# Attention by query tiles of 16 rows and 8 columns over stripes of keys, in a diffusion step kernel

## The chip, the core and the metric

The kernel runs on one NeuronCore of a Trainium2 chip. A core has five engines with instruction queues of their own: TensorE (PE in the profile, its weight loads PEld), VectorE (DVE), ScalarE (ACT), GpSimd (POOL) and SyncE (SP, which here issues every DMA). Each works through its queue in order and waits for the others by semaphores. The metric is the time of one execution on the device in microseconds (us).

## The reference

One layer of a hybrid network, run on 256 context tokens and 1024 latent tokens (a grid of 16 rows of 64), all in float32. Only the attention is touched by the change:

```python
def _neighbourhood_attention(q, k, v, k_ctx, v_ctx, rpb):   # latent queries
    row_start = jnp.clip(r - kh // 2, 0, rows - kh)          # kh = 8 of 16 rows
    row_idx = row_start[:, None] + jnp.arange(kh)[None, :]
    col_start = jnp.clip(c - NA_KW // 2, 0, GRID_W - NA_KW)  # 16 of 64 columns
    col_in = (c[None, :] >= col_start[:, None]) & (c[None, :] < col_start[:, None] + NA_KW)
    s_loc = jnp.einsum('brqhd,brjkhd->bhrqjk', qg, kg).astype(jnp.float32) * scale
    s_loc = jnp.where(col_in[None, None, None, :, None, :],
                      s_loc + bias[None].astype(jnp.float32), NEG_INF)
    s_ctx = jnp.einsum('brqhd,bchd->bhrqc', qg, k_ctx).astype(jnp.float32) * scale
    p = jax.nn.softmax(jnp.concatenate([s_loc.reshape(B, H, rows, GRID_W, n_loc), s_ctx], axis=-1), axis=-1)
    ...
```

There are 8 heads of 64. The latent queries see a window of 8 rows and 16 columns of latent keys and, in the same softmax, 256 cached keys. The context queries see the 256 context keys alone. Around the attention stand one input projection (with the gates of three branches), a pooling and a convolution branch, an output projection and a gated feed-forward part.

## The kernel before

The program has three parts: a front (modulation, norm, the first 18 column units of the input projection and the two small mixers), the attention beside which the remaining 21 units of gate columns are projected, and a rear (output projections and feed-forward).

Float32 products are made of split operands: a high part (`hi`, rounded to the fp32r format) and the rest (`lo`). `products` (L149) issues three matmuls for each piece. A unit of the input projection has 24 pieces: three chunks (512, 512 and 256 tokens) of 8.

In the front, ACT's `evacuate` (L625) copies V (units 6 to 9), K (10 to 13) and Q (14 to 17) out of PSUM into `evac`. V is transposed to token order and stored by `store_tokens` (L316), the latent part once for each of 4 column windows and 2 parities into `v_windows`; K and Q are stored to `kT` and `qT`.

The attention (`attention_engines`, L1104) goes through 80 steps, `s = 10 h + n`: for each head `h` eight latent query tiles (`n` = 0 to 7) of 8 rows and 16 columns, and two tiles of context queries (`n` = 8, 9). Each latent tile sees 12 rows and 32 columns of keys (`LOCAL` = 384) and the 256 cached keys. A step's work is spread over several later steps:

- PE, in step s: `scores(s)` (two local matmuls, L1287, and two for the cached keys, L1292), then half of the gate pieces of this step, `turn(s - 2)` (transposes of the probabilities, L1301), the other gate pieces, `value(s - 3)` (L1315). A step has 5 or 6 gate pieces.
- DVE, in step s: `maximum(s)` (L1448 to L1452), `total(s - 1)` (L1460, L1462), `gather(s - 4)` (L1484), `lower(s - 2)` (L1469), and what is named below.
- ACT, in step s: `gate_out` of a gate chunk that has ended, `exponential(s)` (the cached part, L1367, then the local, L1369), `upper(s - 2)` (L1378), the split of a new weight unit (`split`, L1338).
- POOL, in step s: `normalise(s - 1)` (L1538), the low part of a new weight unit (`lower`, L1514).

`scores(s)` has to wait until DVE has read the local scores of the tile before (`max_step`), and for the cached part until ACT has made its exponentials (`past_ready`): there is one buffer of each.

Between these stand the operations of which each head needs one set. For the next head: KA on ACT (L1344, high part of the keys) and then KB on POOL (L1520, low part) at n = 2 (3 in the first head); QS on ACT (five copies, L1348) and DVE (five, L1432) at n = 5; VV at n = 8; the bias tables on POOL (`tables`, L1531, three additions at n = 4 and three at n = 1). For the output of a head: V stands in the stationary operand with its two parts, so that the output rows come in two halves of the partitions. `lower_rows` (ACT, L1385) copies the second half down to OLO, `add_rows` (DVE, L1490) adds it to OT, and SP stores the sum. This is done at n = 9 for the first 512 tokens, and at n = 4 of the next head for the other 768.

The lines in the loops of ACT and DVE that set this place are the same:

```python
                if n == 9 and h < HEADS:
                    lower_rows(h, 0)
                if n == TIMES + 1 and h > 0:     # TIMES = 3
                    lower_rows(h - 1, 1)
```

## Time and profile before

| | |
|---|---|
| median of 3 runs | 1873.34 us (1871.3 to 1873.45) |
| profiled execution | 1871.09 us, its span 1869.3 us |
| front, to about 330 us | PE busy 320.6 of 330 us |
| attention, 360 to 750 us | PE busy 388.1 of 390 us, DVE 234.8, ACT 222.6, POOL 198.5 |
| rear, 750 to 1869 us | PE busy 1109.7 of 1119 us |
| granted TensorE clock | 1.00 in the attention, 0.998 over the span (2.4 GHz is 1) |

The span runs from the first to the last instruction of the profiled execution. A busy time of PE counts each matmul to its modelled end; since matmuls overlap, the start of one to the start of the next says more than a duration.

### The profile page before, as it was taken

The page shows a single profiled execution, that of the slowest core. Times are in us where ns is not written, and L with a number is a line of the kernel's source. Part 1 is how long each engine was busy: PE and PEld are TensorE (multiplying, and loading weights), DVE is VectorE, ACT ScalarE, POOL GpSimd, SP SyncE. Part 2 cuts the span into 40 slices and gives each one's busy share as a digit, 9 for nine tenths or more (in the row PEclk, how much of TensorE's full clock was granted, in tenths as well). Part 3 has the DMA queues.
Part 4 walks back from the last instruction along what each step waited for, and adds up shares of the span by engine and source line. Part 5 has one row for each costly group of instructions (what it writes and reads, how often), then busy time and mean ns, then how long its engine had stood idle before and what let it go on. Part 6 is the DMA issues. An engine that isn't in the chain of part 4 may idle for free.

```text
span 1869.3 us, 27109 instructions
## 1 busy us (share of the span) xinstructions
PE 1847.3 (99%) x10106; PEld 1587.0 (85%) x10106; DVE 1145.8 (61%) x2142; ACT 758.2 (41%) x1444; POOL 543.7 (29%) x407
## 2 busy tenths in 40 slices
PE   8999999999999999999999999999999999999998
PEld 3788888888888888888888888888888888888898
DVE  4799996156566655366317855554434434789984
ACT  5612232355555564454313522222222222545464
POOL 0000000455555552144532144444344441000000
PEclk9999999999999999999999999999999999999999
DMA  8472545464444532756532222221222224866665
GB/s 325 161 221 62 148 128 192 120 151 115 112 119 112 126 95 75 239 169 185 180 116 68 82 77 96 96 84 58 74 74 74 74 74 150 283 209 224 210 212 204
DMA packets 243466, 260.52 MB, mean 139 GB/s; under 512 B 50696, under 2 KB 182280, under 8 KB 242312
## 3 DMA queue, kind: packets, MB, share of 16 engines
q1 hardware_dynamic: 243336, 258.80, 44.8%
q8 instruction: 81, 1.33, 0.3%
q14 instruction: 49, 0.40, 0.1%
HBM read 196.09 MB, written 62.65 MB: 138 GB/s over the span
## 4 chain that ended last, share of the span: by engine, by line
PE 90%; DVE 4%; DMA 2%; ACT 2%; issue 1%; POOL 0%; SPq 0%; ACTq 0%; DVEq 0%; POOLq 0%
PE ps_all L152 68%; PE ps_all L2452 5%; PE ps_all L2454 4%; PE ps_all L2453 4%; PE ps_all L1315 2%; PE ps_all L1301 2%; DVE mod_acc L825 1%; PE ps_all L1287 1%; DMA wmod_then_mixers<-w_mod_dram 1%; PE ps_all L1292 1%; PE ps_all L537 1%; DMA wmod_block<-w_mod_dram 1%; DVE Y L3114 0%; POOL KB L1520 0%; PE ps_all L2486 0%
## 5 line engine op out<-in xcount | busy, mean ns | idle before, releaser
L152 PE MATMUL ps_all<-AH,w_hi 128*128 128x512 f32 (+1 forms) x1376 | 493.7, 359 | 2.4 <-ACT gate_rows L1360 1.3
L152 PE MATMUL ps_all<-AH,w_lo 128*128 128x512 f32 (+1 forms) x1376 | 483.1, 351 | 0.0
L152 PE MATMUL ps_all<-AL,w_hi 128*128 128x512 f32 (+1 forms) x1376 | 483.0, 351 | 0.0
L152 PEld LDWEIGHTS ps_all<-AH,w_lo 128*128 128x128 f32 x1376 | 259.9, 189 | 36.0
L152 PEld LDWEIGHTS ps_all<-AH,w_hi 128*128 128x128 f32 x1376 | 260.2, 189 | 34.3 <-DVE AL L909 2.0
L152 PEld LDWEIGHTS ps_all<-AL,w_hi 128*128 128x128 f32 x1376 | 260.5, 189 | 30.1
L3033 DVE TENSOR_TENSOR quarter<-ps_all,quarter 128x512 f32<-128x512 f32 x140 | 96.6, 690 | 176.6 <-PE ps_all L152 174.6
L2881 POOL TENSOR_TENSOR slot_lo<-w_pair,slot_hi 128x512 fp32r<-128x512 f32 x96 | 129.9, 1378 | 174.0 <-ACT slot_hi L2654 174.0
L152 PE MATMUL ps_all<-AH,slot_hi 128*128 128x256 f32 (+1 forms) x384 | 129.5, 337 | 0.0
L152 PE MATMUL ps_all<-AL,slot_hi 128*128 128x256 f32 (+1 forms) x384 | 129.2, 336 | 0.0
L152 PE MATMUL ps_all<-AH,slot_lo 128*128 128x256 f32 (+1 forms) x384 | 129.1, 336 | 0.0
L2881 POOL TENSOR_TENSOR w_lo<-w_pair,w_hi 128x512 fp32r<-128x512 f32 x64 | 85.4, 1356 | 114.4 <-ACT w_hi L2654 114.4
L1469 DVE TENSOR_TENSOR PT<-ps_all,PT 128x384 fp32r<-128x384 f32 (+1 forms) x144 | 63.7, 479 | 79.7 <-ACT PT L1378 79.6
L1538 POOL TENSOR_SCALAR prob<-prob,softmax_cols 128x640 f32<-128x640 f32 (+1 forms) x80 | 60.5, 756 | 130.5 <-DVE softmax_cols L1462 125.4
L1367 ACT ACTIVATE prob<-ps_all,softmax_cols 128x256 f32<-128x256 f32 x80 | 38.0, 474 | 137.4 <-DVE softmax_cols L1452 123.9
L845 DVE SCALAR_TENSOR_TENSOR xT_then_mixers<-wmod_then_mixers,cols,xT_then_mixers 128x1295 f32<-128x1295 f32 x60 | 89.4, 1573 | 0.0
L2452 PE MATMUL ps_all<-AH 128*128 128x512 f32 (+1 forms) x248 | 86.9, 350 | 1.1 <-DVE AL L3069 1.1
L1514 POOL TENSOR_TENSOR w_lo<-w_raw,w_hi 128x1024 fp32r<-128x1024 f32 x21 | 50.5, 2404 | 124.6 <-ACT w_hi L1338 124.6
L2454 PE MATMUL ps_all<-AH,AL 128*128 128x512 f32 (+1 forms) x248 | 86.3, 348 | 0.0
L2453 PE MATMUL ps_all<-AL,AH 128*128 128x512 f32 (+1 forms) x248 | 86.3, 348 | 0.0
L2452 PE MATMUL ps_all<-AH,w_hi 128*128 128x512 f32 (+1 forms) x236 | 83.9, 355 | 0.0
L2454 PE MATMUL ps_all<-AH,w_lo 128*128 128x512 f32 (+1 forms) x236 | 83.3, 353 | 0.0
(309 smaller groups left out, 4084.6 us busy)
## 6 DMA issues: line engine op xcount, KB each, us to landing
w_raw<-w_in_dram SPq DMA_DIRECT2D x42, 512.0 KB
w_pair<-w_gu_dram SPq DMA_DIRECT2D x20, 1024.0 KB, 5.3
hidden_in<-hidden SPq DMA_DIRECT2D x77, 256.0 KB, 3.5
wmod_then_mixers<-w_mod_dram SPq DMA_DIRECT2D x19, 1024.0 KB, 8.0
hidden<-quarter SPq DMA_DIRECT2D x50, 256.0 KB, 2.1
branch_and_gates<-gates SPq DMA_DIRECT2D x16, 768.0 KB, 4.4
w_down_rows<-w_down_dram SPq DMA_DIRECT2D x44, 256.0 KB, 3.7
gates<-gate_rows SPq DMA_DIRECT2D x42, 256.0 KB, 2.5
```

Source lines behind the costliest of these rows:

```text
L152: mm = nc.tensor.matmul(out, w, a[:, k, cols[0]:cols[1]], start=(first and part == 0), stop=(last and part == 2))
L845: nc.vector.scalar_tensor_tensor(conv[:, t, :], glu[:, t, k:k + CV], w, conv[:, t, :], ALU.mult, ALU.add).then_inc(conv_step, 1)
L1301: mm = nc.tensor.transpose(psT[:, turned_at(j):turned_at(j) + P], prob[:, s % 3, j * P:(j + 1) * P], g.ident[:, :])
L1367: nc.scalar.activation(pr[:, LOCAL:PCOLS], psS_past, ACT.Exp, bias=c[:, 2:3], accum_out=c[:, 4:5]).then_inc(past_ready, 1)
L1469: nc.vector.tensor_tensor(PT[:, s % 2, j0:j1, P:2 * P], psT[:, turned_at(j0):turned_at(j0) + (j1 - j0) * P].rearrange("p (j n) -> p j n", ...
L1514: nc.gpsimd.tensor_tensor(W.lo[:, u % 2, :], W.raw[:, :], W.hi[:, u % 2, :].bitcast(F32), ALU.subtract).then_inc(W.lo_ready, 1)
L1538: nc.gpsimd.tensor_scalar(pr[:, a:PCOLS], pr[:, a:PCOLS], c[:, 5:6], 1.0, ALU.mult, ALU.mult).then_inc(normal, 1)
L2452: nc.tensor.matmul(out, wh, th, start=first, stop=False)
L2453: nc.tensor.matmul(out, wh, tl, start=False, stop=False)
L2454: return nc.tensor.matmul(out, wl, th, start=False, stop=last)
L2881: nc.gpsimd.tensor_tensor(tiles4(lo), in_pair(p, idx), tiles4(hi.bitcast(F32)), ALU.subtract).then_inc(s_lo, 1)
L3033: nc.vector.tensor_tensor(temp[TEMP[out][side]][:, :], g.ps_all[:, product_bank(p, source), :], temp[TEMP[first][side]][:, :], ALU.add).th ...
```

## The change

Keys, values and queries of the latent tokens are kept in stripe order: stripe w holds the 16 rows of columns 8w to 8w + 7, which are 128 tokens. The front's copy out of PSUM writes this order, so that transposes and stores follow it, and `v_windows` with its eight stores for each V unit is gone. A query tile is one stripe. It sees its own stripe and the neighbours: three blocks of 128 keys, and two for the tiles at the grid's sides (`n` = 0 and 7). The blocks are contiguous in K and V, so QS is made by one copy on ACT and one operation on DVE. There are two bias tables a head instead of six, double buffered, made at n = 6 of the head before; their 16 loads are issued at n = 1 and 2. V holds 12 blocks instead of 20. Since a tile now covers all rows, no half of a head's output is complete before its eighth tile: OT is double buffered, and `lower_rows`, `add_rows` and the store are done in three parts (512, 512 and 256 tokens) at n = 2, 3 and 4 of the next head (the store a step later).

The diff, cut to its core:

```diff
-TROWS, TCOLS = 8, 16
-WROWS, WCOLS = 12, 32
-COL0 = (0, 8, 24, 32)
-KIND = (0, 1, 1, 2)
-KINDS = 3
-SPAN = WCOLS + TCOLS
-WINDOWS = len(COL0) * ROWS * WCOLS // P
-V_CTX, V_PAST = WINDOWS, WINDOWS + CTX // P
+TCOLS = 8
+STRIPES = GW // TCOLS
+REACH = 3 * TCOLS
+V_CTX, V_PAST = STRIPES, STRIPES + CTX // P
 V_BLOCKS = V_PAST + PAST // P
...
-                for n, kc in enumerate(COL0):
-                    for parity in range(2):
-                        sp.dma_start(v_windows[n, parity, :, :, col:col + P], vt[parity * GW + kc:parity * GW + kc + WCOLS, 0:LAT // P, :]).then_inc(tok_stored, 16)
-                sp.dma_start(g.d["v"][LAT:T, col:col + P].rearrange("(t p) n -> p t n", p=P), vt[:, 8:10, :]).then_inc(tok_stored, 16)
+                sp.dma_start(g.d["v"][:, col:col + P].rearrange("(t p) n -> p t n", p=P), vt[:, :, :]).then_inc(tok_stored, 16)
...
-                    nc.scalar.activation(evac[:, u % 2, a:b], ps[:, 0:b - a], ACT.Copy).then_inc(a_free, 1)
+                    if c < 2:
+                        out = evac[:, u % 2, 0:LAT].rearrange("p (s r c) -> p s r c", s=STRIPES, c=TCOLS)[:, :, a // GW:b // GW, :]
+                        nc.scalar.activation(out, ps.rearrange("p (r s c) -> p s r c", s=STRIPES, c=TCOLS), ACT.Copy).then_inc(a_free, 1)
+                    else:
+                        nc.scalar.activation(evac[:, u % 2, a:b], ps[:, 0:b - a], ACT.Copy).then_inc(a_free, 1)
...
-LOCAL = WROWS * WCOLS
+LOCAL = ROWS * REACH
 PCOLS = LOCAL + PAST
-HALVES = ((0, LAT // 2), (LAT // 2, T))
-HALF_TILES = (4, QT)
+PARTS = ((0, LAT // 2), (LAT // 2, LAT), (LAT, T))
+PART_TILES = (STRIPES, STRIPES, QT)
 
 
 def tile_plan(n):
 
-    return divmod(n, len(COL0)) if n < LAT // P else None
+    return [s for s in (n - 1, n, n + 1) if 0 <= s < STRIPES] if n < STRIPES else None
+
+
+def local_at(n):
+
+    return LOCAL - P * len(tile_plan(n))
 
...
-    half, group = plan
-    return [(j, len(COL0) * group + half + j) for j in range(3)], [(3, V_PAST), (4, V_PAST + 1)]
+    return [(3 - len(plan) + j, s) for j, s in enumerate(plan)], [(3, V_PAST), (4, V_PAST + 1)]
...
             def load_b(h, half):
-                if h:
-                    sp.wait_ge(*tables_ready(h - 1, half))
-                else:
-                    sp.wait_ge(b_cleared, half + 1)
-                for r in range(TROWS):
-                    row = TROWS * half + r
+                if half == 0:
+                    if h:
+                        sp.wait_ge(*tables_ready(h - 1))
+                    else:
+                        sp.wait_ge(b_cleared, 1)
+                for row in range(half * ROWS // 2, (half + 1) * ROWS // 2):
                     first = window_start(row)
-                    at = first - half * KH // 2
-                    sp.dma_start(bias_src[r * TCOLS:(r + 1) * TCOLS, half, at:at + KH, :], rpb_rows(g, h, first - row + KH - 1)).then_inc(b_in[half], 16)
...
-                for at, src in ((0, g.v_windows), (V_CTX, g.d["v"][LAT:T, :]), (V_PAST, g.d["cache_v"])):
+                for at, src in ((0, g.d["v"]), (V_PAST, g.d["cache_v"])):
...
-            def store_out(h, half):
-                sp.wait_ge(out_ready, 2 * h + half + 1)
-                a, b = HALVES[half]
-                sp.dma_start(out_rows[h * 64:h * 64 + 64, a:b], OT[0:64, a:b]).then_inc(out_stored, 16)
+            def store_out(h, part):
+                sp.wait_ge(out_ready, 3 * h + part + 1)
+                a, b = PARTS[part]
+                sp.dma_start(out_rows[h * 64:h * 64 + 64, a:b], OT[0:64, h % 2, a:b]).then_inc(out_stored, 16)
...
-                    if n in (1, 4):
-                        load_b(h + 1, n // 4)
+                    if n in (1, 2):
+                        load_b(h + 1, n - 1)
...
-                if n == 9 and h < HEADS:
-                    store_out(h, 0)
-                if n == TIMES + 1 and h > 0:
-                    store_out(h - 1, 1)
+                if h > 0 and n in (3, 4, 5):
+                    store_out(h - 1, n - 3)
...
-                at = 2 * plan[1] + plan[0] if plan else n
-                q = QS[:, b, at * P:(at + 1) * P]
+                q = QS[:, b, n * P:(n + 1) * P]
                 if plan:
-                    r0, c0 = plan[0] * KH // 2, COL0[plan[1]]
                     if s:
                         pe.wait_ge(max_step, 2 * b0(s))
                     for m, K in enumerate((KA, KB)):
-                        keys = K[:, b, 0:LAT].rearrange("p (r c) -> p r c", c=GW)[:, r0:r0 + WROWS, c0:c0 + WCOLS]
-                        nc.tensor.matmul(psS_local.rearrange("p (i j) -> p i j", j=WCOLS), q, keys, start=(m == 0), stop=(m == 1))
+                        nc.tensor.matmul(psS_local[:, local_at(n):LOCAL], q, K[:, b, plan[0] * P:(plan[-1] + 1) * P], start=(m == 0), stop=(m == 1))
                 k0 = T if plan else LAT
...
-                    for out, src in by_tiles(QS[:, b, :], kq_src):
-                        nc.scalar.activation(out, src, ACT.Copy, scale=DH ** -0.5).then_inc(q_hi, 1)
+                    nc.scalar.activation(QS[:, b, :], kq_src[:, 0:T], ACT.Copy, scale=DH ** -0.5).then_inc(q_hi, 1)
...
-            def lower_rows(h, half):
-                act.wait_ge(summed_v, h * QT + HALF_TILES[half])
-                if 2 * h + half:
-                    act.wait_ge(out_ready, 2 * h + half)
-                a, b = HALVES[half]
-                nc.scalar.activation(OLO[:, 0:b - a], OT[64:P, a:b], ACT.Copy).then_inc(olo_ready, 1)
+            def lower_rows(h, part):
+                act.wait_ge(summed_v, h * QT + PART_TILES[part])
+                if 3 * h + part:
+                    act.wait_ge(out_ready, 3 * h + part)
+                a, b = PARTS[part]
+                nc.scalar.activation(OLO[:, 0:b - a], OT[64:P, h % 2, a:b], ACT.Copy).then_inc(olo_ready, 1)
...
-                if n == 9 and h < HEADS:
-                    lower_rows(h, 0)
-                if n == TIMES + 1 and h > 0:
-                    lower_rows(h - 1, 1)
-            lower_rows(HEADS - 1, 1)
+                if h > 0 and n in (2, 3, 4):
+                    lower_rows(h - 1, n - 2)
+            lower_rows(HEADS - 1, 2)
 
...
-                half, group = plan
-                if group == 0:
-                    dve.wait_ge(*tables_ready(s // QT, half))
+                h, a = s // QT, local_at(n)
+                if n == 0:
+                    dve.wait_ge(*tables_ready(h))
+                seen = bias[:, b, 1, P:LOCAL] if n == 0 else bias[:, b, 1, 0:2 * P] if n == STRIPES - 1 else bias[:, b, 0, :]
                 nc.vector.tensor_reduce(c[:, 1:2], psS_past, AX, ALU.max).then_inc(max_step, 1)
-                nc.vector.tensor_tensor_reduce(prob[:, s % 3, 0:LOCAL], psS_local, bias[:, half, KIND[group], :],
+                nc.vector.tensor_tensor_reduce(prob[:, s % 3, a:LOCAL], psS_local[:, a:LOCAL], seen,
...
-            def add_rows(h, half):
-                a, b = HALVES[half]
-                rows = OT[0:64, a:b]
-                dve.wait_ge(olo_ready, 2 * h + half + 1)
+            def add_rows(h, part):
+                a, b = PARTS[part]
+                rows = OT[0:64, h % 2, a:b]
+                dve.wait_ge(olo_ready, 3 * h + part + 1)
...
-                if n == 9 and h < HEADS:
-                    add_rows(h, 0)
-                if n == TIMES + 1 and h > 0:
-                    add_rows(h - 1, 1)
-            add_rows(HEADS - 1, 1)
+                if h > 0 and n in (2, 3, 4):
+                    add_rows(h - 1, n - 2)
+            add_rows(HEADS - 1, 2)
 
...
-            def tables(h, half):
-                pool.wait_ge(b_in[half], 16 * TROWS * (h + 1))
-                if h:
-                    pool.wait_ge(max_step, 2 * (b0((h - 1) * QT + 4 * half + 3) + 1))
-                for kind in range(KINDS):
-                    seen = bias_src[:, half, :, TCOLS // 2 * kind:TCOLS // 2 * kind + WCOLS]
-                    nc.gpsimd.tensor_tensor(bias[:, half, kind, :].rearrange("p (i j) -> p i j", j=WCOLS), seen[:, :, ::-1],
-                                            col_mask[:, kind, :].rearrange("p (a j) -> p a j", a=1).broadcast_to([P, WROWS, WCOLS]), ALU.add).then_inc(table_ready, 1)
+            def tables(h):
+                b = h % 2
+                pool.wait_ge(b_in, 16 * ROWS * (h + 1))
+                if h >= 2:
+                    pool.wait_ge(max_step, 2 * (h - 1) * NL)
+                seen = bias_src[:, :, ::-1].rearrange("p r (s c) -> p s r c", c=TCOLS)
+                for kind in range(2):
+                    mask = col_mask[:, kind, :].rearrange("p (s a c) -> p s a c", a=1, c=TCOLS).broadcast_to([P, 3, ROWS, TCOLS])
+                    nc.gpsimd.tensor_tensor(bias[:, b, kind, :].rearrange("p (s r c) -> p s r c", r=ROWS, c=TCOLS), seen, mask, ALU.add).then_inc(table_ready, 1)
 
...
-                if n == 1 and 0 < h < HEADS:
-                    tables(h, 1)
                 if h + 1 < HEADS:
                     if n == (2 if h else 3):
                         prepare("k", h + 1)
-                    elif n == 4:
-                        tables(h + 1, 0)
+                    elif n == 6:
+                        tables(h + 1)
                     elif n == 8:
                         prepare("v", h + 1)
```

On ACT, these rows are from the place in the second head (h = 1, counted from 0) where KA is made: before, from the exponentials of n = 2 to those of n = 4.

```order
L1367 ACTIVATE prob,softmax_cols<-ps_all,softmax_cols 128x256
L1369 ACTIVATE prob,softmax_cols<-prob,softmax_cols 128x384
L1378 ACTIVATE PT<-ps_all 128x3x128
L1378 ACTIVATE PT<-ps_all 128x2x128
L1344 ACTIVATE KA<-kq_src 128x1536
L1367 ACTIVATE prob,softmax_cols<-ps_all,softmax_cols 128x256
L1369 ACTIVATE prob,softmax_cols<-prob,softmax_cols 128x384
L1378 ACTIVATE PT<-ps_all 128x3x128
L1378 ACTIVATE PT<-ps_all 128x2x128
L1360 ACTIVATE gate_rows<-ps_all,cols 128x256
L1367 ACTIVATE prob,softmax_cols<-ps_all,softmax_cols 128x256
```

And in the changed kernel at the same place:

```order
L1353 ACTIVATE prob,softmax_cols<-ps_all,softmax_cols 128x256
L1356 ACTIVATE prob,softmax_cols<-prob,softmax_cols 128x384
L1365 ACTIVATE PT<-ps_all 128x2x128 x2
L1331 ACTIVATE KA<-kq_src 128x1536
L1372 ACTIVATE OLO<-OT 64x512
L1353 ACTIVATE prob,softmax_cols<-ps_all,softmax_cols 128x256
L1356 ACTIVATE prob,softmax_cols<-prob,softmax_cols 128x384
L1365 ACTIVATE PT<-ps_all 128x3x128
L1365 ACTIVATE PT<-ps_all 128x2x128
L1372 ACTIVATE OLO<-OT 64x512
L1346 ACTIVATE gate_rows<-ps_all,cols 128x256
L1353 ACTIVATE prob,softmax_cols<-ps_all,softmax_cols 128x256
```

A copy to OLO stands right behind KA, another behind `upper` of the next step, and the third behind the split of a weight unit (where one falls there).

On DVE, before, the same head from the maximum of n = 3 to that of n = 4:

```order
L1469 TENSOR_TENSOR PT<-ps_all,PT 128x3x128
L1469 TENSOR_TENSOR PT<-ps_all,PT 128x2x128
L1448 TENSOR_REDUCE softmax_cols<-ps_all 128x1
L1449 ISA prob,softmax_cols<-ps_all,bias 128x384
L1449 ISA softmax_cols 128x1
L1452 TENSOR_SCALAR softmax_cols<-softmax_cols 128x1
L1460 TENSOR_TENSOR softmax_cols<-softmax_cols 128x1
L1462 RECIPROCAL softmax_cols<-softmax_cols 128x1
L1484 TENSOR_REDUCE OT<-ps_all 128x128
L1469 TENSOR_TENSOR PT<-ps_all,PT 128x3x128
L1469 TENSOR_TENSOR PT<-ps_all,PT 128x2x128
L1448 TENSOR_REDUCE softmax_cols<-ps_all 128x1
```

And in the changed kernel from the addition at the end of n = 2 to the maximum of n = 4:

```order
L1472 TENSOR_TENSOR OT<-OT,OLO 64x512
L1432 TENSOR_REDUCE softmax_cols<-ps_all 128x1
L1433 ISA prob,softmax_cols<-ps_all,bias 128x384
L1433 ISA softmax_cols 128x1
L1436 TENSOR_SCALAR softmax_cols<-softmax_cols 128x1
L1444 TENSOR_TENSOR softmax_cols<-softmax_cols 128x1
L1446 RECIPROCAL softmax_cols<-softmax_cols 128x1
L1466 TENSOR_REDUCE OT<-ps_all 128x128
L1453 TENSOR_TENSOR PT<-ps_all,PT 128x3x128
L1453 TENSOR_TENSOR PT<-ps_all,PT 128x2x128
L1472 TENSOR_TENSOR OT<-OT,OLO 64x512
L1432 TENSOR_REDUCE softmax_cols<-ps_all 128x1
```

The addition to OT now stands ahead of the maximum of n = 3 and again ahead of that of n = 4, where before nothing stood between `lower` (PT) and the maximum (L1448, L1432 in the changed kernel). On POOL, KB stays behind the one normalisation of n = 2; the three table additions that stood ahead of it in n = 1 are gone.

## Rows read from the trace of the kernel before

**Rows 1.** Busy time by engine, the page, whole span.

```profile
PE 1847.3 (99%) x10106; PEld 1587.0 (85%) x10106; DVE 1145.8 (61%) x2142; ACT 758.2 (41%) x1444; POOL 543.7 (29%) x407
```

**Rows 2.** Timeline of PE: start, duration, engine, line, operation, operands.

```profile
403.67 0.71 PE L1301 MATMUL ps_all<-ident,prob 128*128 128x128 f32 x5
...
409.55 0.38 PE L1301 MATMUL ps_all<-ident,prob 128*128 128x128 f32 x2
...
411.86 0.76 PE L1315 MATMUL ps_all<-PT,VV 128*128 128x256 f32 x5
412.45 0.34 PE L1287 MATMUL ps_all<-KA,QS 128*128 128x384 f32 x1
...
412.81 0.28 PE L1292 MATMUL ps_all<-KA,QS 128*128 128x256 f32 x1
```

**Rows 3.** Timeline of PE, step n = 5 of h = 0, transposes of n = 3.

```profile
384.85 0.33 PE L1301 MATMUL ps_all<-ident,prob 128*128 128x128 f32 x1 [1.06 <-POOL prob L1538]
```

**Rows 4.** Timeline of ACT, POOL and DVE, h = 1, n = 2 and 3.

```profile
420.31 1.49 ACT L1344 ACTIVATE KA<-kq_src 128x1536 fp32r<-128x1536 f32 x1
...
420.99 0.41 DVE L1448 TENSOR_REDUCE softmax_cols<-ps_all 128x1 f32<-128x256 f32 x1
...
421.88 3.49 POOL L1520 TENSOR_TENSOR KB<-kq_src,KA 128x1536 fp32r<-128x1536 f32 x1 [1.56 <-ACT KA L1344]
...
422.04 3.35 DVE L1460 TENSOR_TENSOR softmax_cols<-softmax_cols 128x1 f32<-128x1 f32 x1
...
422.16 0.48 ACT L1367 ACTIVATE prob<-ps_all,softmax_cols 128x256 f32<-128x256 f32 x1 [0.36 <-DVE softmax_cols L1452]
...
423.23 0.75 ACT L1378 ACTIVATE PT<-ps_all 128x384 fp32r<-128x384 f32 x2
```

**Rows 5.** Timeline of POOL and DVE at the end of h = 0.

```profile
406.06 2.40 POOL L1514 TENSOR_TENSOR w_lo<-w_raw,w_hi 128x1024 fp32r<-128x1024 f32 x1 [0.23 <-ACT w_hi L1338]
...
406.66 2.34 DVE L1490 TENSOR_TENSOR OT<-OT,OLO 64x512 f32<-64x512 f32 x1 [0.98 <-ACT OLO L1385]
408.93 0.41 DVE L1448 TENSOR_REDUCE softmax_cols<-ps_all 128x1 f32<-128x256 f32 x1
```

**Rows 6.** Groups by line of ACT, 340 to 750 us.

```profile
L1385 ACT ACTIVATE OLO<-OT 64x512 f32<-64x512 f32 x8 | 5.0, 631 | 0.2
```

**Rows 7.** Timeline of ACT and PE, start of h = 1, n = 7.

```profile
440.55 0.48 ACT L1367 ACTIVATE prob<-ps_all,softmax_cols 128x256 f32<-128x256 f32 x1 [2.26 <-DVE softmax_cols L1452]
...
441.17 0.38 PE L1292 MATMUL ps_all<-KA,QS 128*128 128x256 f32 x1 [0.22 <-ACT prob L1367]
```

**Rows 8.** Timeline of PE, scores of the cached keys, n = 4 of four heads.

```profile
425.37 0.28 PE L1292 MATMUL ps_all<-KA,QS 128*128 128x256 f32 x1
...
521.90 0.28 PE L1292 MATMUL ps_all<-KA,QS 128*128 128x256 f32 x1
...
568.40 0.28 PE L1292 MATMUL ps_all<-KA,QS 128*128 128x256 f32 x1
...
616.58 0.28 PE L1292 MATMUL ps_all<-KA,QS 128*128 128x256 f32 x1
```

**Rows 9.** Timeline of ACT and POOL, n = 2 and 3 of heads 2 to 5.

```profile
468.56 2.41 POOL L1514 TENSOR_TENSOR w_lo<-w_raw,w_hi 128x1024 fp32r<-128x1024 f32 x1 [1.13 <-ACT w_hi L1338]
...
515.38 1.49 ACT L1344 ACTIVATE KA<-kq_src 128x1536 fp32r<-128x1536 f32 x1
...
565.24 3.50 POOL L1520 TENSOR_TENSOR KB<-kq_src,KA 128x1536 fp32r<-128x1536 f32 x1 [2.14 <-ACT KA L1344]
...
611.88 3.50 POOL L1520 TENSOR_TENSOR KB<-kq_src,KA 128x1536 fp32r<-128x1536 f32 x1 [1.45 <-ACT KA L1344]
...
614.72 1.06 ACT L1338 ACTIVATE w_hi<-w_raw 128x1024 fp32r<-128x1024 f32 x1
```

**Rows 10.** Timeline of PE, the same scores, h = 5, n = 5.

```profile
622.46 0.28 PE L1292 MATMUL ps_all<-KA,QS 128*128 128x256 f32 x1
```

**Rows 11.** Groups by line of POOL, whole span.

```profile
L1531 POOL TENSOR_TENSOR bias<-bias_src,col_mask 128x384 f32<-128x384 f32 x48 | 51.4, 1099 | 2.0 <-DMA bias_src<-rpb_dram 2.0
```

More of the change, by code:

```diff
@@ L1118, in attention_engines @@
         VV = sb("VV", [P, 2, V_BLOCKS, 2 * DH], FR)
[L1119 to L1120 removed]
+        bias = sb("bias", [P, 2, 2, LOCAL])
+        col_mask = sb("col_mask", [P, 2, REACH])
         prob = sb("prob", [P, 3, PCOLS])
         PT = sb("PT", [P, 2, 5, 2 * P], FR)
[L1123 to L1124 removed]
+        OT = sb("OT", [P, 2, T])
+        OLO = sb("OLO", [64, LAT // 2])
         st = sb("softmax_cols", [P, 4, 6])
@@ L1250, in sync @@
                         load_w(u + 3)
-            store_out(HEADS - 1, 1)
-            sp.wait_ge(out_stored, 16 * 2 * HEADS)
+            for part in (1, 2):
+                store_out(HEADS - 1, part)
+            sp.wait_ge(out_stored, 16 * len(PARTS) * HEADS)
             for b in range(2):
@@ L1368, in exponential @@
                 if plan:
-                    nc.scalar.activation(pr[:, 0:LOCAL], pr[:, 0:LOCAL], ACT.Exp, bias=c[:, 2:3], accum_out=c[:, 3:4]).then_inc(local_ready, 1)
+                    a = local_at(s % QT)
+                    nc.scalar.activation(pr[:, a:LOCAL], pr[:, a:LOCAL], ACT.Exp, bias=c[:, 2:3], accum_out=c[:, 3:4]).then_inc(local_ready, 1)
             def upper(s):
@@ L1540, in gpsimd @@
             lower(1)
-            pool.wait_ge(mask_in, 16 * KINDS)
-            for half in range(2):
-                nc.gpsimd.memset(bias_src[:, half, :, :], NEG).then_inc(b_cleared, 1)
+            pool.wait_ge(mask_in, 16)
+            nc.gpsimd.memset(bias_src[:, :, :], NEG).then_inc(b_cleared, 1)
+            nc.gpsimd.memset(col_mask[:, 1, :], 0.0).then_inc(b_cleared, 1)
             prepare("k", 0)
-            tables(0, 0)
             lower(2)
-            tables(0, 1)
+            pool.wait_ge(b_cleared, 2)
+            tables(0)
             for s in range(STEPS_END):
@@ L1583, in rpb_rows @@
     rows, width = 2 * KH - 1, 2 * GW - 1
-    return bass.AP(tensor=rpb.tensor, offset=rpb.offset + (h * rows + first) * width + WCOLS,
-                   ap=[[1, TCOLS], [width, KH], [1, SPAN]])
+    return bass.AP(tensor=rpb.tensor, offset=rpb.offset + (h * rows + first) * width + GW - KW,
+                   ap=[[1, TCOLS], [width, KH], [1, REACH]])
 RCH = ((0, 512), (512, LAT), (LAT, T))
```

53 lines of the change are left out of this document (19 added, 34 removed).

## The prediction, as it was put on record before the changed kernel ran

> **What bounds the kernel now.** I read the busy times first. TensorE (PE) is busy 1847.3 of 1869.3 us [rows 1], so at most 22 us of waits can be won back; any larger gain has to take work out of PE's queue. Next the waits of PE: in the attention stage they are few, the longest the wait for a normalised tile in the first head, 1.06 us beyond the modelled end of the matmul before it [rows 3]. So while PE runs through, the stage costs what its matmuls cost, start to start. Then the timelines of DVE, ACT and POOL around one head, because they say how near each hand-over comes to making PE wait. The reader should see a loop there. PE's scores of a tile need the maximum (DVE) and the exponential of the cached part (ACT) of the tile before. From the start of a maximum to the start of its exponential it takes 422.16 - 420.99 = 1.17 us [rows 4], the exponential 0.48, and PE starts 441.17 - 441.03 = 0.14 us after its end [rows 7]: 1.79 us together. In front of a maximum, whatever else stands in DVE's queue is added.
>
> **A lock between DVE and POOL.** In the same timeline, L1460 adds two columns of one element and takes 3.35 us, from 422.04 to 425.39. POOL's KB runs from 421.88 to 425.37 [rows 4]. Likewise the addition to OT takes 2.34 us while w_lo runs on POOL to 408.46, and DVE's next instruction starts at 408.93, that is 0.47 us after POOL's end [rows 5]. An addition of two SBUF operands on DVE does not start before the POOL instruction that is running has ended; it then takes 0.47 us for 64x512. The exponentials on ACT beside it show no such stretch (0.48 us at 422.16).
>
> The Trainium skill has this as a rule (SBUF — State Buffer, section "SBUF: two separate sides"): DVE instructions with two SBUF inputs and GpSimd instructions that read SBUF share one pair of ports, taken for a whole instruction by whoever is first. The rule speaks against this change, and the trace agrees with it (3.35 us for one element a partition). If it did not hold at the new place, the sum below would lose its 8.8 us of new waits and come out as the first rival.
>
> **What goes from PE.** The side tiles n = 0 and n = 7 see two blocks of keys instead of three: 16 tiles of 64. For each:
> - two local matmuls of 256 columns instead of 384. With 384 the start-to-start time is (412.81 - 412.45) / 2 = 0.18 us, with 256 it is (0.76 - 0.28) / 4 = 0.12 [rows 2]. Saved 2 x 0.06 = 0.12.
> - one transpose less: (0.71 - 0.38) / 3 = 0.11 [rows 2].
> - one value matmul of 256 columns less: 0.12.
>
> That is 0.35 us, and for 16 tiles 5.6 us, all on the path. The other 48 tiles have as many columns as before. That their keys are now contiguous brings nothing that the rows could show: 384 strided columns cost 0.18 us, 1.5 times the 0.12 of 256 contiguous ones. Bound: 0 to 0.01 us each.
>
> **An old wait that shrinks.** In the first head PE waits before the transposes of n = 3 because POOL's normalisation stands behind KB, and KB behind a chain that begins with the low part of V [rows 3]. V has 12 blocks instead of 20, so VV on ACT and POOL is shorter by some 40%, and the key load that waits for it is issued a good microsecond earlier. I count 1.0 of the 1.06 us as won (0 to 1.1).
>
> **What the new place of OLO and OT costs.** Before, the pair stood at n = 9 and n = 4. Now it stands at n = 2, 3 and 4. At n = 2 the copy to OLO comes right behind KA on ACT, and POOL starts KB as soon as KA has ended: KA ends at 421.80, KB starts at 421.88 [rows 4]. The copy takes 0.63 us [rows 6], so the addition to OT comes to DVE some 0.6 us after KB has taken the ports, and waits for the whole of KB (3.5 us). Behind it on DVE stands the maximum of n = 3, behind this its exponential on ACT, and PE's scores of n = 4 wait for both. So PE can start the cached scores of n = 4 at KB's end + 0.47 + 1.79 = KB's end + 2.26. In the trace of before, they started [rows 8]:
> - h = 1: 425.37, KB ended 425.37: late by 2.26 us.
> - h = 3: 521.90. KA ended 515.38 + 1.49 = 516.87 [rows 9]; KB was held up then by table additions that are gone now, so it starts about 516.95, ends 520.45, and PE could start at 522.71: 0.81.
> - h = 4: 568.40, KB ended 568.74: 2.60.
> - h = 5: 616.58, KB ended 615.38: 1.06.
> - h = 2 (and h = 6, which looks the same): w_lo runs on POOL over the end of KA, to 470.97 [rows 9]. The addition to OT is asked for before that end and KB only after it, so it goes first: no wait. h = 7 has no KA.
>
> Sum 6.7 us. The same thing can happen at n = 3 and 4 with w_lo, where the split of a weight unit stands just ahead of OLO. In h = 5 the split fell in n = 3 [rows 9]. Carried on from there: OT ends 615.85, the exponential of n = 3 starts 617.02, the copy of PT 1.07 later [rows 4] and ends 618.84, split (1.06) to 619.9, OLO to 620.5; w_lo holds the ports from 620.0 to 622.4, OT ends 622.9, and PE's cached scores of n = 5 can start at 624.7. They would stand at 622.46 [rows 10] + 1.06: another 1.1 us. After such a stretch DVE is behind, and the copies to QS at n = 5 come before it has caught up; in h = 1 of before PE waited for this at n = 7 (the row at 441.17 is that place [rows 7]), and I expect the same once more in h = 5: 1.0 us (0 to 1.5). Together 8.8 us.
>
> **Edits that I count at nothing.** The copies out of PSUM in the front write runs of 8 columns; ACT has waits for PE before each of them, and PE's four banks cover several us. Fewer stores of V and fewer bytes of tables are off the path. One copy and one operation for QS instead of five and five save instruction overheads but no longer overlap; about even. Two tables a head instead of six relieve POOL by some 4 x 1.1 us a head [rows 11], where it mostly waited; should runs of 8 cost more than 1.1 us each, up to 2 us, a normalisation near them could come late (0 to 2 us in all). The 16 loads of bias rows in a row keep SP for some 8 us; a gate store behind them has longer than that until its buffer is needed again, and the weight load too.
>
> **Sum.** -5.6 - 1.0 + 8.8 = +2.2 us against the profiled execution of 1871.09 us (span 1869.3, and 1.8 us around it): 1873.3 us. This execution stands 2.25 us below the median of the runs shown, 1873.34, so I put the median of the changed kernel at 1875.5 us. What a measurement can tell from no change is about 0.2% or 3.7 us; the forecast lies inside.
>
> **Rivals.**
> A. *The new waits don't come about, and PE's savings remain.* The addition to OT would have to reach DVE before KB takes the ports, or DVE to reach the maximum in another way. For it: the order is a matter of 0.6 us, and in two of the six heads it goes this way. Against: ACT's queue puts KA before OLO in every head, and in four heads POOL stood idle waiting for KA. -5.6 - 1.0, with about 1 us of waits left over: 1867 to 1869 us. Chance 0.2.
> B. *The lag does not heal.* One mechanism: KB wins the ports in heads 2 and 6 as well, and each time DVE then reaches the QS copies of n = 5 late, so that PE waits again at n = 7. It decides from the point at which POOL's next instruction takes the ports directly after w_lo although DVE has asked before. Price: 2 heads x 1.7 us (the mean of the four above), and 1.0 us at n = 7 in four more heads: +7.4 on top of +2.2, some 1883 us at the most; half of it, about 1880, is its likeliest. For it: DVE's timeline has little air in n = 2 to 5, where three additions now stand instead of one. Against: rows 5 show DVE getting the ports when POOL's instruction ends. Chance 0.3.
> C. *SP is late.* The bias loads keep a gate store back until ACT waits for its buffer, and PE for ACT. It would cost up to 2 us a head, 1885 us. For it: sixteen issues in a row in some heads. Against: two chunks of gates lie between. Chance 0.03.
>
> **How the numbers follow.** The forecast, 1872 to 1879 us, has 0.47. Range for 8 in 10: the low end takes in A (1867), the high end most of B (1881). Faster by over 0.2% (below 1869.6): A without its upper edge, 0.18. Slower by over 0.2% (above 1877.1): B, C and the upper edge of the forecast, 0.37. Within: 0.45.
>
> **What would show it.** In the changed kernel's profile: the transposes and value matmuls of n = 0 and 7 four in a row instead of five; the first addition to OT in heads 1, 3, 4 and 5 with some 3.5 us instead of 0.6, ending 0.5 us after KB; PE waits for DVE or ACT before the scores of n = 4 in these heads, 2.3, 0.8, 2.6 and 1.1 us, and none in heads 2 and 6. PE's busy time over the span lower by some 5 to 6 us while its idle time is higher by 7 to 9. The forecast is wrong if the first additions to OT are short (A), if PE's waits before n = 7 appear in most heads (B), or if ACT waits for the gate stores (C). A front that takes longer would show that the copies in stripes were not free.

## The result, and the profile of the changed kernel

The changed kernel takes 1878.97 us (median of 9 runs, 1877.17 to 1880.71), the kernel before 1873.34 (9 runs beside it, 1870.45 to 1874.72): ratio 1.0032, 95% interval 1.0023 to 1.0041. It is slower by 5.6 us, clear of no change; the forecast was 2.2 us, to 1875.5, which could not have been told from no change. The profiled execution took 1878.09 us, with a span of 1876.2 against 1869.3 before. Its three parts, from the first and the last matmul of the attention stage:

| part | before | after | difference |
|---|---|---|---|
| up to the stage | 359.9 | 359.2 | -0.7 |
| attention stage | 390.3 | 396.3 | +6.0 |
| behind it | 1119.1 | 1120.7 | +1.6 |

The last row is not the change's. Behind the stage the code is the same; TensorE's granted clock fell to 0.5 there for some 3.4 us in this execution and not in the profiled one of before. The nine times of before fit this as something that comes and goes: four lie at 1870.5 to 1871.5 us, five at 1873.3 to 1874.7; but only one execution of each kernel is traced. Without that 1.6 us the profile has +5.4 us, near the medians' 5.6, and all of it is in the attention stage. The front's 0.7 us tells nothing: with the same code it ends between 358.7 and 361.1 us in the nine traces of changed kernels. The busy times:

```profile
PE 1848.3 (99%) x10074; PEld 1583.2 (84%) x10074; DVE 1139.3 (61%) x2118; ACT 750.2 (40%) x1420; POOL 497.4 (27%) x375
```

PE has fewer matmuls and yet is busy 1 us longer [rows 1]: a part of its work ran slower. PE's waits, first of before and then of after, in the attention stage (engine, line, what was waited for: us in total, times, longest):

```profile
PE ps_all L1301 <- POOL prob L1538: 1.1, 1, 1.1
...
PE ps_all L1301 <- DVE PT L1469: 0.4, 1, 0.4
PE ps_all L1292 <- ACT prob L1367: 0.4, 2, 0.2
```

```profile
PE ps_all L1274 <- DVE softmax_cols L1433: 5.2, 6, 2.1
PE ps_all L1279 <- ACT prob L1353: 1.8, 7, 0.3
...
PE ps_all L1288 <- DVE PT L1453: 0.8, 2, 0.4
```

The wait for POOL is gone, and a wait for VectorE's maximum has come. Its place in head 1, in the timelines of ACT, POOL, DVE and PE (start, duration, engine, line, operation; in brackets the idle time before it and what ended it):

```profile
417.34 1.49 ACT L1331 ACTIVATE KA<-kq_src 128x1536 fp32r<-128x1536 f32 x1
418.86 0.63 ACT L1372 ACTIVATE OLO<-OT 64x512 f32<-64x512 f32 x1
...
418.91 3.50 POOL L1500 TENSOR_TENSOR KB<-kq_src,KA 128x1536 fp32r<-128x1536 f32 x1 [2.04 <-ACT KA L1331]
...
419.52 3.44 DVE L1472 TENSOR_TENSOR OT<-OT,OLO 64x512 f32<-64x512 f32 x1 [1.54 <-ACT OLO L1372]
422.88 0.41 DVE L1432 TENSOR_REDUCE softmax_cols<-ps_all 128x1 f32<-128x256 f32 x1
...
424.66 0.58 PE L1279 MATMUL ps_all<-KA,QS 128*128 128x256 f32 x1 [0.22 <-ACT prob L1353]
```

As in [rows 4, 5], the addition waits for POOL: KB ends at 422.41, the maximum starts 0.47 us later, and the cached scores of n = 4 start at 424.66, that is KB's end + 2.25. The same in head 4, where the wait is longest (PE, two stretches of its timeline):

```profile
567.36 0.63 PE L1302 MATMUL ps_all<-PT,VV 128*128 128x256 f32 x4
570.06 0.45 PE L1274 MATMUL ps_all<-KA,QS 128*128 128x384 f32 x1 [2.06 <-DVE softmax_cols L1433]
...
571.27 0.63 PE L147 MATMUL ps_all<-AH,w_hi 128*128 128x512 f32 x1
571.70 0.63 PE L147 MATMUL ps_all<-AL,w_hi 128*128 128x512 f32 x1
...
575.67 0.40 PE L147 MATMUL ps_all<-AL,w_hi 128*128 128x512 f32 x1
575.90 0.40 PE L147 MATMUL ps_all<-AH,w_lo 128*128 128x512 f32 x1
```

The maximum is late by 2.2 us for PE. Behind the wait the gate's matmuls of 512 columns follow each other at 571.70 - 571.27 = 0.43 us, from 575.67 on at 0.23 again. The windows view shows why (stretch, its length, busy time and count of PE, PEld, DVE, ACT, POOL, then the granted clock, DMA share, GB/s):

```profile
420.00:424.00 4.00, 2.27 (x13) 1.76 (x12) 3.96 (x6) 0.00 (x0) 2.41 (x1) 1.00 0.10 18
424.00:428.00 4.00, 3.78 (x11) 2.87 (x11) 2.90 (x10) 2.92 (x8) 0.80 (x1) 0.57 0.71 186
570.00:574.50 4.50, 4.22 (x12) 3.22 (x13) 3.34 (x13) 2.91 (x8) 0.80 (x1) 0.63 0.74 192
```

Right behind the two longest waits of the stage, in heads 1 and 4, the granted clock is at its lower level, 1.2 GHz, for about 3.4 us (0.57 and 0.63 are means over the stretches). In the stage of before it is 1.00 throughout. Not every execution of the changed kernel has both falls: over the span, seven of the nine have a mean granted clock of 0.995 or 0.996, and two have 0.998. That is at most 2 x 0.0025 x 1875.4 = 9.4 us at the lower level, of which the end of the program takes 5.0 to 6.7 us in all ten traces, so that one such stretch at most is left. These two took 1877.17 and 1877.55 us, the lowest.

I summed over the stage what each matmul's start-to-start time is above its usual one (differences over 0.095 us; good to some 0.5 us, since it hangs on what is called usual): 3.6 us before, 15.8 after. Of the 12.2 us more, 2.7 are matmuls at half the clock, and 9.5 are waits. -5.6 + 9.5 + 2.7 = +6.6, against +6.0 measured for the stage. A part of the 0.6 us between them is that the first local product of 384 columns now takes 0.176 us to the start of the next, with contiguous keys, where it took 0.181 (medians over the stage); the prediction had bounded this by 0.01 us.

### The profile page after: what moved, and what is told of

Its sections match the earlier page's. It is cut to its first block, busy times and chain, and to the rows that moved or that the text cites. A ratio compares the mean times of both kernels' runs of the same rounds, so it can differ in the third digit from the quotient of the medians.

```text
span 1876.2 us, 26924 instructions
## 1 busy us (share of the span) xinstructions
PE 1848.3 (99%) x10074; PEld 1583.2 (84%) x10074; DVE 1139.3 (61%) x2118; ACT 750.2 (40%) x1420; POOL 497.4 (27%) x375
## 4 chain that ended last, share of the span: by engine, by line
PE 89%; DVE 3%; ACT 3%; issue 3%; DMA 1%; POOL 0%; SPq 0%; ACTq 0%; DVEq 0%
PE ps_all L147 68%; PE ps_all L2431 4%; PE ps_all L2432 4%; PE ps_all L2433 4%; PE ps_all L1302 2%; PE ps_all L1288 1%; PE ps_all L1279 1%; PE ps_all L528 1%; PE ps_all L1274 1%; DMA wmod_block<-w_mod_dram 1%; DVE prob L1433 1%; PE ps_all L432 1%; ACT prob L1356 0%; DVE Y L3093 0%; DVE softmax_cols L1432 0%
## 5 line engine op out<-in xcount | busy, mean ns | idle before, releaser
L1453 DVE TENSOR_TENSOR PT<-ps_all,PT 128x256 fp32r<-128x256 f32 (+1 forms) x144 | 61.5, 464 | 80.2 <-ACT PT L1365 80.2
L1519 POOL TENSOR_SCALAR prob<-prob,softmax_cols 128x640 f32<-128x640 f32 (+2 forms) x80 | 57.1, 714 | 172.4 <-DVE softmax_cols L1446 172.4
```

Of the source, the lines that this page charges most:

```text
L1453: nc.vector.tensor_tensor(PT[:, s % 2, j0:j1, P:2 * P], psT[:, turned_at(j0):turned_at(j0) + (j1 - j0) * P].rearrange("p (j n) -> p j n", ...
L1519: nc.gpsimd.tensor_scalar(pr[:, a:PCOLS], pr[:, a:PCOLS], c[:, 5:6], 1.0, ALU.mult, ALU.mult).then_inc(normal, 1)
```

## Experiments

Each run stands beside runs of the kernel before on the same chip; ratios are to these. The first four shared one set (median 1873.04 us), the last four another (1872.09); beside the changed kernel it was 1873.34, so that up to 1.3 us between runs of different sets is not theirs.

**The copy ahead of KA** (olo_before_ka).

```
+                if h > 0 and n in (2, 3, 4):
+                    lower_rows(h - 1, n - 2)
                 if h + 1 < HEADS:
                     if n == (2 if h else 3):
                         prepare("k", h + 1)
 ...
-                if h > 0 and n in (2, 3, 4):
-                    lower_rows(h - 1, n - 2)
```

> The changed kernel with one line moved: on ScalarE the copy of the lower rows of a finished piece of the output stands ahead of the copy of the next head's keys to KA instead of behind it (the copy of a weight chunk, the split, still stands ahead of both). Theory: in the changed kernel VectorE's addition to OT waits for POOL's KB, 3.4 us, and with it the cached scores of n=4 (heads 1, 3, 4, 5: 2.6 + 1.0 + 2.7 + 1.1 = 7.4 us of gaps in its trace); with the copy first the addition runs beside KA and is over before KB starts. The two stretches at half the clock behind the longest gaps (1.7 us each) go as well. 1879.0 - 7.4 - 3.4 = 1868, range 1866 to 1871. Still there: the two gaps of head 5 at n=5 and n=7, about 1 us each, where POOL's w_lo stands behind the split. Rival 1: the gaps come from the load of three additions on VectorE in the head's first steps, wherever the copy stands: the time stays at 1877 to 1880. Rival 2: the gaps go but the clock falls somewhere else: about 1871.5.

Measured: 1869.06 us, ratio 0.9977 (0.9967 to 0.9987), 9.9 us below the changed kernel and inside the range. The waits at n = 4 and the two falls of the clock are gone. DVE and POOL at the place of the 3.44 us above:

```profile
418.01 0.68 DVE L1472 TENSOR_TENSOR OT<-OT,OLO 64x512 f32<-64x512 f32 x1 [0.17 <-ACT OLO L1372]
418.62 0.41 DVE L1432 TENSOR_REDUCE softmax_cols<-ps_all 128x1 f32<-128x256 f32 x1
...
419.67 3.43 DVE L1444 TENSOR_TENSOR softmax_cols<-softmax_cols 128x1 f32<-128x1 f32 x1
...
419.57 3.51 POOL L1500 TENSOR_TENSOR KB<-kq_src,KA 128x1536 fp32r<-128x1536 f32 x1 [2.84 <-ACT KA L1331]
```

VectorE loses the same 3.4 us to KB. But it is the total of the tile that waits, with the maximum done, as it was in the kernel before [rows 4]. So the order next to KA is the cause of the waits at n = 4, not the load of three additions. What I had not seen: in head 1 the third addition, behind the split of n = 4, waits for w_lo, and VectorE carries this lag past the operation for QS to n = 7:

```profile
429.33 2.28 DVE L1472 TENSOR_TENSOR OT<-OT,OLO 64x256 f32<-64x256 f32 x1 [0.78 <-ACT OLO L1372]
...
435.71 1.49 DVE L1416 SCALAR_TENSOR_TENSOR QS<-kq_src,QS 64x1280 fp32r<-64x1280 f32 x1 [0.55 <-ACT QS L1334]
```

PE waits 1.0 us for it before the scores of n = 7, and 1.3 more in the steps up to the next transposes.

**The copy ahead of the split too** (olo_before_all).

```
+                if h > 0 and n in (2, 3, 4):
+                    lower_rows(h - 1, n - 2)
                 for u in units_freed(s - 1):
                     if 0 < u <= BESIDE - 2:
                         split(u + 2)
 ...
-                if h > 0 and n in (2, 3, 4):
-                    lower_rows(h - 1, n - 2)
```

> As the run before, but the copy of the lower rows stands ahead of the split too, directly behind the copy to PT. Theory: the additions to OT now start before either of POOL's subtractions (KB, w_lo), so that the gap of head 5 at n=5 (0.9 us) goes too: 1867, range 1865 to 1870; most of what the gap gave back is 1 us, about as much as the measurement tells. Rival: the copy, 0.63 us, now delays the split and with it w_lo and the gate's first product of a chunk: no better than the run before, or 1 us worse.

Measured: 1863.40 us, ratio 0.9951 (0.9938 to 0.9963), below my range: 5.7 us below the run before. The stage takes 383.1 instead of 386.8 us. Another 1.6 us between the two profiled executions is the fall of the clock behind the stage, which this one doesn't have; that the medians differ by it too is likely and not shown. The third addition in head 1 is over before w_lo starts:

```profile
428.67 0.41 DVE L1472 TENSOR_TENSOR OT<-OT,OLO 64x256 f32<-64x256 f32 x1
```

So w_lo costs in this kernel as KB does. I had given it 1 us.

**Side tiles with three stripes again** (side_tiles_padded), otherwise the kernel just above.

```
-    return [s for s in (n - 1, n, n + 1) if 0 <= s < STRIPES] if n < STRIPES else None
+    return [s + min(max(n - 1, 0), STRIPES - 3) for s in range(3)] if n < STRIPES else None
 ...
-                seen = bias[:, b, 1, P:LOCAL] if n == 0 else bias[:, b, 1, 0:2 * P] if n == STRIPES - 1 else bias[:, b, 0, :]
+                seen = bias[:, b, 1 if n in (0, STRIPES - 1) else 0, :]
```

> The kernel of the run before (copy ahead of the split and of KA) with the first and the last query tile of each head seeing three stripes again, as in the kernel before; the mask's columns do not fit these tiles, so that their probabilities are other numbers, and only the time is read. Theory: TensorE works without a gap in this stage, so that the work that the side tiles save is saved in full: 16 tiles x 0.35 us = 5.6 us more than the run before, 1872.6, range 1870 to 1875, which is the time of the kernel before. Rival: the side tiles' steps are bound by VectorE or ScalarE and the saved products are hidden: the same time as the run before within 1 us.

Measured: 1869.12 us, ratio 0.9976 (0.9968 to 0.9985), 5.7 us above the kernel with short side tiles, where 5.6 were expected; the time itself is below my range, because the kernel that it starts from was. The medians' difference may hold a fall of the clock behind the stage, which this profiled execution has and the other has not. The stages alone, 387.2 and 382.8 us, differ by 4.4 us, and the longer one has 0.9 us less of waits, so that PE's work is some 5.3 us. The saving comes in almost whole, and the rival, that it is hidden, is out.

**Work in the two longest waits** (fill_the_wait), the changed kernel otherwise.

```
+                if s in (14, 44):
+                    for m in range(14):
+                        nc.tensor.matmul(psV[s % 2][:, 2 * P:4 * P], KA[:, b, 0:P], KA[:, b, 0:2 * P], start=True, stop=True)
                 if plan:
```

> The changed kernel with 14 products of 128x256 (about 0.11 us each, 1.6 us in all) put on TensorE ahead of the scores of n=4 in heads 1 and 4 alone, where it waits for 2.6 us; they write a part of the output bank that nothing reads. Theory: the clock falls to half for 3.4 us behind these two waits because TensorE stood still; with work in the wait the clock stays up, the gaps stay where they are, and 2 x 1.7 us come back: 1879.0 - 3.4 = 1875.6, range 1874.5 to 1877. Rival 1: the fall has another cause (it follows the stage, not the wait): the granted clock of these stretches is still 0.5 and the time stays at 1879, or rises up to 3 us by the products. Rival 2: the gaps are short enough that the products push the scores back by themselves: 1877 to 1880.

Measured: 1877.55 us, ratio 1.0025 (1.0016 to 1.0034), 1.4 us below the changed kernel and just above my range, where rival 2 stood. PE in the first of the two places, and the two stretches in the windows view:

```profile
422.35 1.84 PE L1272 MATMUL ps_all<-KA 128*128 128x256 f32 x14
424.25 0.44 PE L1277 MATMUL ps_all<-KA,QS 128*128 128x384 f32 x1
```

```profile
424.00:428.00 4.00, 3.71 (x21) 2.77 (x19) 2.87 (x11) 2.92 (x8) 0.80 (x1) 1.00 0.81 197
570.00:574.50 4.50, 3.88 (x20) 3.02 (x20) 3.37 (x11) 2.92 (x8) 0.80 (x1) 1.00 0.73 178
```

The clock stays up: its fall followed from PE standing still. Rival 2, that the products push the scores back, is out: from the start of KB to the scores of n = 4 in head 1 it takes 4.90 us here (419.35 to 424.25) and 4.91 in the changed kernel (418.91 to 423.82), and in head 4 PE still waits 0.40 us behind the products. Yet the stage is only 0.5 us shorter (395.8). PE now reaches n = 7 earlier, and VectorE, late by the lag of n = 4, doesn't:

```profile
440.99 0.39 PE L1277 MATMUL ps_all<-KA,QS 128*128 128x256 f32 x1 [0.71 <-DVE softmax_cols L1436]
...
441.83 0.39 PE L1282 MATMUL ps_all<-KA,QS 128*128 128x256 f32 x1 [0.34 <-ACT prob L1356]
```

The waits at n = 7 of head 1 grow from 0.7 to 2.2 us, and head 4 gets 0.9 us where it had none. These 2.4 us are near the clock's 2.7: the half-speed matmuls stood in place of these waits. So the clock's 2.7 us are not an addition that could be had back by themselves: the lag of VectorE would have cost nearly as much.

**The addition behind the maximum** (add_behind_max); ScalarE's order is the changed kernel's.

```
                 if s < STEPS:
                     maximum(s)
+                if h > 0 and n in (3, 4, 5):
+                    add_rows(h - 1, n - 3)
                 if 0 <= s - 1 < STEPS:
                     total(s - 1)
 ...
-                if h > 0 and n in (2, 3, 4):
-                    add_rows(h - 1, n - 2)
```

> The changed kernel with ScalarE's order as it is (the copy of the lower rows behind the split and KA), but on VectorE the addition to OT stands one step later and behind the maximum of the tile instead of ahead of it. The addition still waits for POOL's KB, about 3.4 us. Theory: what costs is not that something on VectorE waits for POOL but that the maximum stands behind it; now the maximum goes first and the gaps before the scores of n=4 are gone, with the stretches at half the clock: as with the copy moved ahead on ScalarE, 1864 to 1869 us, 1867 the likeliest. Rival: the wait only moves one step on, to the scores of n=5, since the total, the gathering and the lower parts of PT stand behind the addition: 1873 to 1879.

Measured: 1862.94 us, ratio 0.9947 (0.9935 to 0.9960), 1 us below my range. The addition waits as long as ever, and PE for nothing of it (DVE and POOL in heads 1 and 2, then all waits of PE in the stage):

```profile
418.49 3.51 POOL L1501 TENSOR_TENSOR KB<-kq_src,KA 128x1536 fp32r<-128x1536 f32 x1 [2.04 <-ACT KA L1331]
419.10 3.45 DVE L1472 TENSOR_TENSOR OT<-OT,OLO 64x512 f32<-64x512 f32 x1 [0.39 <-ACT OLO L1372]
...
465.39 3.50 POOL L1501 TENSOR_TENSOR KB<-kq_src,KA 128x1536 fp32r<-128x1536 f32 x1
465.43 4.00 DVE L1472 TENSOR_TENSOR OT<-OT,OLO 64x512 f32<-64x512 f32 x1
```

```profile
PE ps_all L147 <- ACT gate_rows L1346: 0.8, 2, 0.4
```

This is the clearest of the runs: 3.45 us of waiting cost PE 2.4 us at n = 4 of head 1 with the maximum behind them, and nothing with the maximum ahead. In head 2, KB even goes ahead of the addition here, which is rival B's condition, and the addition takes 4.00 us without a wait of PE.

**Both moves** (both_orders).

> Both moves: the copy of the lower rows ahead of the split and of KA on ScalarE, the addition to OT behind the maximum on VectorE. Theory: the copy alone brought 1863.4, and in its trace the gap that is left in this stage is 1.6 us in head 5 at n=7. Behind the maximum the addition meets KB and w_lo again, in which VectorE's total of the tile now waits anyway; each is some 0.6 us nearer to the normalisation on POOL. I expect 1863 to 1865, no gain over the copy alone beyond 1 us. Rival: the additions queue behind KB together with the total, and the normalised tile comes late for the transposes: 1866 to 1870.

Measured: 1863.29 us, ratio 0.9953 (0.9940 to 0.9967), as either move alone. The stage has two waits of 0.6 to 0.7 us before transposes, and little else.

**The three parts at n = 6, 7 and 8** (parts_at_678), the loops' `n in (2, 3, 4)` and the stores moved on by four.

> The changed kernel with the three copies to OLO and additions to OT at n=6, 7 and 8 instead of 2, 3 and 4, the stores with them; the order within a step as in the changed kernel. Theory: the place next to KA costs, and there is none at n=6 to 8 (the split can fall there); but the additions now stand behind the copies for QS of n=5, where VectorE is late in every kernel so far, so that gaps before n=7 and n=8 come: 1866 to 1872, 1869 the likeliest. Rival: the three additions load VectorE by the same amount wherever they stand: 1877 or more.

Measured: 1862.09 us, ratio 0.9946 (0.9934 to 0.9959), the lowest median of all; it can't be told from add_behind_max. It is 7 us below the likeliest of my forecast and 4 below its range. The waits that I expected behind QS did not come; the largest of PE's in the stage before a score is 0.34 us. In head 1 the first two additions take 1.12 and 0.68 us, the third 1.57, behind a split at n = 8. That VectorE was late at n = 6 and 7 in the other kernels came, it seems, for the most part from the additions at n = 2 to 4, but no run parts this from the rest.

**An addition of 8 columns** (add_of_8_columns).

```
-                rows = OT[0:64, h % 2, a:b]
+                rows = OT[0:64, h % 2, a:a + 8]
 ...
-                nc.vector.tensor_tensor(rows, rows, OLO[:, 0:b - a], ALU.add).then_inc(out_ready, 1)
+                nc.vector.tensor_tensor(rows, rows, OLO[:, 0:8], ALU.add).then_inc(out_ready, 1)
```

> The changed kernel with each addition to OT cut to 64x8 elements instead of 64x512 and 64x256; the other columns of the output lack their lower half. Theory (the operation does not start before POOL's has ended): the first addition of heads 1, 3, 4 and 5 still takes about 3 us or more, until KB has ended, and then 0.1 instead of 0.47 us; the gaps before n=4 stay but for 0.4 us each: 1876 to 1878. Rival (the two share the bandwidth, and a small operation gets through): the addition takes 0.2 us, the gaps before n=4 are gone: 1865 to 1870.

Measured: 1871.94 us, ratio 0.9998 (0.9990 to 1.0007). The size of the time is missed by 4 us; the mechanism is as expected (DVE and POOL, head 1):

```profile
420.15 2.91 DVE L1472 TENSOR_TENSOR OT<-OT,OLO 64x8 f32<-64x8 f32 x1 [1.54 <-ACT OLO L1372]
...
419.55 3.50 POOL L1500 TENSOR_TENSOR KB<-kq_src,KA 128x1536 fp32r<-128x1536 f32 x1 [2.04 <-ACT KA L1331]
```

An addition of 8 columns that takes 0.16 us elsewhere ends only with KB, at 423.06 and 423.05. The waits at n = 4 stay, shorter by the 0.5 us that the columns cost: 1.37 instead of 1.89 us before the scores of head 1, 1.69 instead of 2.22 in head 4. The clock falls behind the second and not behind the first. The stage is 4.6 us shorter, where I had counted 0.4 us for each of four heads and left out the clock and the additions at n = 3 and 4. Of the remaining 2.4 us between the two medians, 1.3 are between the sets (1873.34 and 1872.09 for the kernel before); the rest I can't place from one profile of each.

## Why the prediction was near, and which term was too small

- **-5.6 us on PE: right.** The timeline has the short tiles, 256 columns for the scores at n = 0 and four value matmuls where there were five [rows 2], and the padded run gives 5.7 us by its median, some 5.3 by the two stages:

```profile
404.33 0.28 PE L1274 MATMUL ps_all<-KA,QS 128*128 128x256 f32 x1
...
409.62 0.34 PE L1274 MATMUL ps_all<-KA,QS 128*128 128x384 f32 x1
...
421.45 0.63 PE L1302 MATMUL ps_all<-PT,VV 128*128 128x256 f32 x4
```

- **-1.0 us for the first head: right**, 1.2 us. The transposes follow without idle time [rows 3]:

```profile
382.61 0.71 PE L1288 MATMUL ps_all<-ident,prob 128*128 128x128 f32 x5
```

- **The new waits at n = 4: right in place and cause**, 6.7 us forecast. To the start of the cached scores, as the prediction counts, they are late in heads 1, 3, 4, 5 by 2.4, 0.8, 2.7, 1.2 us, together 7.2, against 2.3, 0.8, 2.6, 1.1. In heads 2 and 6 the addition asks while w_lo runs and goes ahead of KB, without a wait of PE, so rival B's condition did not hold in this kernel:

```profile
470.18 0.97 DVE L1472 TENSOR_TENSOR OT<-OT,OLO 64x512 f32<-64x512 f32 x1 [2.50 <-ACT OLO L1372]
...
470.56 3.96 POOL L1500 TENSOR_TENSOR KB<-kq_src,KA 128x1536 fp32r<-128x1536 f32 x1
```

- **Head 5, n = 5 and n = 7: right**, 0.9 and 1.2 us for 1.1 and 1.0, counted in the same way. The addition of n = 3 takes 2.33 us with w_lo beside it.
- **"Together 8.8 us": too small.** This is the term that was off. Waits net of those of before rose by 9.5 us, with the first head's gain of 1.2 in it, so the new ones are 10.7; and 2.7 us more went by at half the clock behind the waits of heads 1 and 4. Together that is 13.4 us where the prediction had 8.8. Of the 10.7, the places named above have 9.3 (7.2 + 0.9 + 1.2); the rest are small ones that I had left out: 0.3 us more at n = 7 of head 3, 0.2 and 0.5 before transposes in heads 3 and 6, and 0.1 at a time where PE starts again. I had priced a wait of PE at its own length, and let VectorE's lag bring a new wait at n = 7 in head 5 alone. The runs show that such a wait also brings slow matmuls behind it (fill_the_wait), and that VectorE's lag, to which the third addition adds in heads 1 and 4 (2.28 us each, w_lo beside it), is paid at one of the two places: as half-speed matmuls in the changed kernel, as waits at n = 7 with the clock kept up. In this, rival B's heading, the lag does not heal, was partly true, though its way there was not.
- **PE's busy time lower by 5 to 6 us, its idle time higher by 7 to 9: neither came.** The two stages in the windows view, before and after (the fields are those above):

```profile
359.90:750.20 390.30, 388.32 (x2362) 345.15 (x2360) 234.80 (x689) 222.80 (x574) 198.50 (x156) 1.00 0.44 113
359.20:755.60 396.40, 388.52 (x2330) 341.27 (x2329) 228.79 (x668) 215.04 (x553) 156.19 (x128) 0.99 0.37 100
```

  Idle time rises from 2.0 to 7.9 us, and busy time by 0.2: the half-speed matmuls, and those drawn out beside a wait, count as busy and hide the 5.6 us that are saved.
- **The number.** The mechanism was right, and the result lies in the range, but some luck is in that: a net of 2.2 us is the difference of two larger terms, and the new cost missed by half of itself makes the change 2.5 times as large as forecast. The time lies at the upper edge of the forecast's own 1872 to 1879 us.
- **Edits counted at nothing: right as far as the trace tells.** Tables of 8-column runs take 1056 ns each, not more than before [rows 11], and there are 16 instead of 48. The front is not longer. ACT's waits in the stage are for DVE, PE and loads, none for a gate's store (rival C).

```profile
L1513 POOL TENSOR_TENSOR bias<-bias_src,col_mask 128x384 f32<-128x384 f32 x16 | 16.6, 1056 | 4.9 <-DMA bias_src<-rpb_dram 4.9
```

Rival A, no new waits, is what the moved lines give: I put it at 1867 to 1869 us, and the four orders in which PE hardly waits run at 1862.1 to 1863.4. I had left 1 us of waits in it and had not counted that before's other waits would go as well, 2.4 us beside the first head's 1.2, among them 1.2 at n = 7 of head 1 [rows 7]. The stage of parts_at_678 takes 381.4 us, 8.9 less than before's 390.3, where 5.6 of work and 3.6 of waits make 9.2. How much of this the kernel before would gain with only its own addition moved is open: I did not run it.

## What to carry to other kernels

When an instruction is moved next to one that starts a long POOL subtraction, ask first what stands behind it on VectorE. Here a lock of 3.4 us cost nothing when the operation that PE's next matmul needs was already out, and 0.8 to 2.7 us when that operation queued behind. And a wait of PE of 2 us is not priced by its length alone: look at the granted clock behind it, and at whether the engine that was late has caught up at its next heavy place. The two costs don't simply add: with the clock kept up, 0.5 us of 2.7 came back.

## What the runs showed of the hardware

- An addition on VectorE of two SBUF operands, of 1 element, 8 or 512 columns, ends within 0.6 us after the POOL subtraction that was running when it was asked for; its size sets only that last part. The Trainium skill says the same (SBUF — State Buffer, "SBUF: two separate sides"): the pair of ports is locked for a whole instruction. All three sizes agree with it.
- TensorE's granted clock fell to 1.2 GHz for about 3.4 us behind waits of 2.22, 1.89 and 1.69 us, and not behind one of 1.37 us or where the wait held 14 small matmuls. These are single executions, and the times of others say that the falls are not in all of them.
- Behind the stage the code is the same in all ten kernels. Five of the ten traces have such a fall there, at the end of a row of one-column matmuls or within 1 us behind it: it costs 1.6 us where it lasts 3.4 us, and 3.2 where it lasts 6.8 (add_behind_max). What brings it isn't shown. Two executions that differ by this amount say nothing of the kernel.
